# A depthwise convolution shared out anew among TensorE, VectorE, ScalarE and GpSimd

## What is computed

```python
def conformer_conv(h, w_pw1, b_pw1, w_dw, b_dw, ln_g, ln_b, w_pw2, b_pw2):
    u = h @ w_pw1 + b_pw1
    a, gate = jnp.split(u, 2, axis=-1)
    u = a * jax.nn.sigmoid(gate)
    u = lax.conv_general_dilated(          # depthwise, causal, width 31
        u, w_dw[:, None, :], window_strides=(1,), padding=[(CONV_WIDTH - 1, 0)], ...) + b_dw
    u = jax.nn.silu(layernorm(u, ln_g, ln_b))
    return u @ w_pw2 + b_pw2
```

## Time and profile before

| | us |
|---|---|
| median of 3 runs | 1820.41 (1819.27 to 1821.78) |
| span of the profiled execution | 1817.7 |
| TensorE busy in the span | 1765.9 (97%) |
| VectorE busy | 1029.6 (57%) |
| ScalarE busy | 707.8 (39%) |
| GpSimd busy | 172.1 (9%) |

### The profile page before, as it was taken

One profiled execution on the slowest core, in us unless ns is written; L12 is line 12 of the kernel. 1 busy time (PEld: TensorE's weight loads), 2 busy tenths in 40 slices (PEclk: granted clock), 3 DMA queues, 4 the chain that ended last, 5 costly groups with the idle time before them and its releaser, 6 DMA issues.

```text
span 1817.7 us, 21121 instructions
## 1 busy us (share of the span) xinstructions
PE 1765.9 (97%) x8106; PEld 1404.2 (77%) x8106; DVE 1029.6 (57%) x1287; ACT 707.8 (39%) x1095; POOL 172.1 (9%) x128
## 2 busy tenths in 40 slices
PE   7999799999999999999999999989999899999997
PEld 6887588888888878778888888756557778888886
DVE  6998664433444555654424444559856677537753
ACT  5655532212233344332212323465564444324431
POOL 0010010000000100110000004471200200000001
PEclk9999999999999999999999999999999999999998
DMA  5210322322232311132312231523112122322221
GB/s 181 70 47 28 99 94 101 115 95 83 102 118 78 124 70 53 65 105 103 127 70 93 92 127 70 153 73 116 50 62 70 70 93 101 119 70 92 101 96 47
DMA packets 28052, 164.63 MB, mean 91 GB/s; under 512 B 4511, under 2 KB 5675, under 8 KB 11596
## 3 DMA queue, kind: packets, MB, share of 16 engines
q1 hardware_dynamic: 25088, 158.11, 24.7%
q10 hardware_dynamic: 2892, 5.55, 1.0%
HBM read 156.28 MB, written 4.47 MB: 88 GB/s over the span
## 4 chain that ended last, share of the span: by engine, by line
PE 88%; DVE 8%; ACT 2%; issue 1%; POOL 1%; DMA 0%; DVEq 0%; SPq 0%; ACTq 0%; POOLq 0%
PE PS L620 26%; PE PS L622 26%; PE PS L621 26%; PE PS L726 1%; PE PS L727 1%; PE PS L725 1%; DVE W_lo L1821 1%; DVE WK L2266 1%; DVE SSUM L2307 1%; DVE TOP L2264 1%; PE PS L1045 1%; ACT W_hi L1154 1%; POOL ISC L1765 1%; PE PS L1056 1%; DVE PS L2443 0%
## 5 line engine op out<-in xcount | busy, mean ns | idle before, releaser
L620 PE MATMUL PS<-H_hi,W_hi 128*128 128x512 f32 x1600 | 641.6, 401 | 18.3 <-DVE H_lo L1801 14.0
L622 PE MATMUL PS<-H_hi,W_lo 128*128 128x512 f32 x1600 | 626.1, 391 | 0.0
L621 PE MATMUL PS<-H_lo,W_hi 128*128 128x512 f32 x1600 | 625.6, 391 | 0.0
L1154 ACT ACTIVATE W_hi<-W_raw 128x2048 fp32r<-128x2048 f32 (+2 forms) x130 | 262.6, 2020 | 674.2 <-PE PS L622 674.2
L620 PEld LDWEIGHTS PS<-H_hi,W_hi 128*128 128x128 f32 x1600 | 301.9, 189 | 105.1 <-issue 41.2
L1821 DVE TENSOR_TENSOR W_lo<-W_raw,W_hi 128x2048 fp32r<-128x2048 f32 (+2 forms) x130 | 331.2, 2548 | 59.5 <-ACT W_hi L1154 59.1
L622 PEld LDWEIGHTS PS<-H_hi,W_lo 128*128 128x128 f32 x1600 | 301.5, 188 | 64.6
L621 PEld LDWEIGHTS PS<-H_lo,W_hi 128*128 128x128 f32 x1600 | 302.2, 189 | 59.5 <-issue 1.2
L620 PE MATMUL PS<-HID_hi,W_hi 128*128 128x512 f32 x640 | 250.3, 391 | 7.5 <-DVE HID_lo L1962 7.4
L622 PE MATMUL PS<-HID_hi,W_lo 128*128 128x512 f32 x640 | 249.7, 390 | 0.0
L621 PE MATMUL PS<-HID_lo,W_hi 128*128 128x512 f32 x640 | 249.7, 390 | 0.0
(11 more groups left out here) (289 smaller groups left out, 1522.0 us busy)
## 6 DMA issues: line engine op xcount, KB each, us to landing
W_raw<-in_inp SPq DMA_DIRECT2D x13, 1024.0 KB, 4.8
W_raw<-in_pw SPq DMA_DIRECT2D x11, 1024.0 KB, 4.8
W_raw<-in_gu0a SPq DMA_DIRECT2D x11, 1024.0 KB, 4.8
W_raw<-in_gu0b SPq DMA_DIRECT2D x11, 1024.0 KB, 4.8
W_raw<-in_gu1a SPq DMA_DIRECT2D x11, 1024.0 KB, 4.8
W_raw<-in_gu1b SPq DMA_DIRECT2D x11, 1024.0 KB, 4.8
W_raw<-in_gu2a SPq DMA_DIRECT2D x11, 1024.0 KB, 4.8
W_raw<-in_gu2b SPq DMA_DIRECT2D x11, 1024.0 KB, 4.8
```

The lines of the kernel that those rows point to most:

```text
L620: nc.tensor.matmul(dst[:], wh, x_hi[:, k, :], start=(k == first), stop=False)
L621: nc.tensor.matmul(dst[:], wh, x_lo[:, k, :], start=False, stop=False)
L622: return nc.tensor.matmul(dst[:], wl, x_hi[:, k, :], start=False, stop=(k == last))
L1154: nc.scalar.activation(W_hi[b][:, 0:n], W_raw[b][:, 0:n], ACT.Copy).then_inc(w_hi, 1)
```

## The change

The taps are shared by three engines. `PE_TILES` gives TensorE 66 taps: tile 1 whole, the last 9 of tile 5, the last 26 of tile 7. VectorE has 124: tiles 0, 3, 4 and 6 whole. GpSimd has 58 (`POOL_TAPS`): tile 2 whole, 22 of tile 5, 5 of tile 7.

- VectorE's two sums lie in PSUM, in AUX[2] and AUX[3]; only the last tap of a tile writes CV. TensorE's tiles take turns in AUX[0] and AUX[1], and the third waits until the first is copied out.
- For 55 of GpSimd's 58 taps ScalarE makes the product (`scaled_tap`, into one of four buffers TAP in SBUF) and GpSimd adds it to CV. For a tile's tap 0 GpSimd multiplies and adds the bias itself. ScalarE waits for `pool_tap`, the tap four back, before it overwrites a buffer.
- The scaled taps have places in ScalarE's queue by slot (`SCALED_AT`): ten of them between two sigmoids, from slot 50 on; the last four stand ahead of diagonal chunk 9.
- TensorE takes its first tap at slot 64 and one behind every second slot: 32 taps inside the units, 34 behind them, with `bias_products` behind tap 55. The sums of tiles 5, 6 and 7 for the mean are separate matmuls.
- GpSimd's queue: taps of tile 2, mean sums of tiles 0, 2, 3 (it waits for tile 3 of VectorE), taps of tile 5, mean sums of tiles 1 and 4, taps of tile 7.
- `DVE_TAPS` is [5, 8, 9, 16, 16, 16, 16]; behind the last U come 1 tap, `conv_lo`, 20 taps, the join of tile 5, 17 taps, the join of tile 7. `conv_lo` of tile 5 comes in unit 5, that of tile 7 behind the last U.

```diff
-PE_TILES = [(1, 0), (3, 0), (5, 6), (7, 10)]
+PE_TILES = [(1, 0), (5, 22), (7, 5)]
-DVE_TILES = [(0, 31), (2, 31), (4, 31), (5, 6), (6, 31), (7, 10)]
-DVE_TAPS = [5, 8, 21, 24, 24, 24, 24]
+DVE_TILES = [0, 3, 4, 6]
+DVE_TAPS = [5, 8, 9, 16, 16, 16, 16]
+POOL_TILES = [(2, CONV_WIDTH), (5, 22), (7, 5)]
+SCALED = [n for n, (m, t) in enumerate(POOL_TAPS) if t]
-FIRST_TAP = 48
+FIRST_TAP, TAPS_INSIDE = 64, 32
+CHUNK_AT = {g: c for c, g in enumerate([40, 46, 52] + [FIRST_TAP + 2 * CHUNK * (c - 2) for c in range(3, 8)])}
+TAKE_AT = FIRST_TAP + 2 * PE_ENDS[0] + 1
+SCALED_AT = [50 + 3 * k // 2 for k in range(30)] + [101 + 3 * k // 2 for k in range(18)]
-        CVacc = T_hid
+        TAP = [SQ[:, 0, :], SQ[:, 1, :], STD[:], T_hid[:]]
...
+            def scaled_tap(k):
+                n = SCALED[k]
+                m, t = POOL_TAPS[n]
+                if t == 1:
+                    act.wait_ge(glu_made, m + 1)
+                if k >= len(TAP):
+                    act.wait_ge(pool_tap, SCALED[k - len(TAP)] + 1)
+                nc.scalar.activation(TAP[k % len(TAP)], U[:, m, t:t + SEQ], ACT.Copy,
+                                     scale=vec("w_dw", t * DT + m)).then_inc(act_scaled, 1)
...
+            def taps(x):
+                m, end = POOL_TILES[x]
+                for n in range(POOL_ENDS[x] - end, POOL_ENDS[x]):
+                    t = POOL_TAPS[n][1]
+                    if t == 0:
...
+                        nc.gpsimd.tensor_scalar(CV[:, m, :], U[:, m, 0:SEQ], vec("w_dw", m), vec("b_dw", m),
+                                                ALU.mult, ALU.add).then_inc(pool_tap, 1)
+                        continue
+                    k = SCALED.index(n)
+                    pool.wait_ge(act_scaled, k + 1)
+                    pool.wait_ge(pool_tap, n)
+                    nc.gpsimd.tensor_tensor(CV[:, m, :], CV[:, m, :], TAP[k % len(TAP)], ALU.add).then_inc(pool_tap, 1)
...
             def conv(count, upto):
...
-                    dst = (CV[:, m, :], CVacc[:])[t % 2]
+                    acc = AUX[2 + t % 2][:]
...
-                        i = nc.vector.scalar_tensor_tensor(out=dst, in0=src, scalar=w, in1=dst, op0=ALU.mult, op1=ALU.add)
+                        dst = CV[:, m, :] if t == CONV_WIDTH - 1 else acc
+                        i = nc.vector.scalar_tensor_tensor(out=dst, in0=src, scalar=w, in1=acc, op0=ALU.mult, op1=ALU.add)
...
             conv(1, DT)
-            conv_lo(3)
-            conv(9, DT)
-            conv_joined(2)
+            conv_lo(2)
+            conv(20, DT)
+            conv_join(1)
             conv(len(todo), DT)
-            conv_joined(3)
+            conv_join(2)
```

More of the change, by code:

```diff
@@ L378, in build @@
         r_copied = sem("r_copied")
-        y_scaled = sem("y_scaled")
-        t_pool = sem("t_pool")
+        act_scaled = sem("act_scaled")
+        pool_tap = sem("pool_tap")
         x_pool = sem("x_pool")
@@ L720, in conv_tap @@
                     pe.wait_ge(r_copied, COPIED_NORMS.index(MIX0) + 1)
+                    if p == 2:
+                        pe.wait_ge(conv_pe_taken, 1)
                 if x == 0:
@@ L754, in _ @@
                             token_spread(AUX[1], r_ps)
-                        if g >= FIRST_TAP:
-                            conv_tap(g - FIRST_TAP)
-            for n in range(SLOTS * L.n - FIRST_TAP, len(PE_TAPS)):
+                        if g >= FIRST_TAP and g % 2 == 0:
+                            conv_tap((g - FIRST_TAP) // 2)
+            for n in range(TAPS_INSIDE, len(PE_TAPS)):
                 conv_tap(n)
-            bias_products()
-            pe.wait_ge(ln_sum, 7)
+                if n == 55:
+                    bias_products()
+            pe.wait_ge(acc_free, L.n)
+            pe.wait_ge(ln_sum, len(MEAN_POOL) - 1)
             nc.tensor.matmul(PS[0][:], ones, SSUM[:], start=True, stop=False)
-            pe.wait_ge(conv_made, 6)
+            pe.wait_ge(conv_made, MADE.index(5) + 1)
+            nc.tensor.matmul(PS[0][:], ones, CV[:, 5, :], start=False, stop=False)
+            pe.wait_ge(conv_made, MADE.index(6) + 1)
+            nc.tensor.matmul(PS[0][:], ones, CV[:, 6, :], start=False, stop=False)
+            pe.wait_ge(conv_made, MADE.index(7) + 1)
             nc.tensor.matmul(PS[0][:], ones, CV[:, 7, :], start=False, stop=True).then_inc(ln_sum_ready, 1)
@@ L1287, in beside_pw1 @@
                         split_hi(act, L, At(j - 1))
-                    if j - 1 in (1, 3, 5):
-                        conv_hi((j - 2) // 2)
+                    if j - 1 in (1, 5):
+                        conv_hi((j - 1) // 4)
                 if g in CHUNK_AT:
                     diagonals(CHUNK_AT[g])
-                if g in TAKE_AT:
-                    take_conv(TAKE_AT[g])
+                if g == TAKE_AT:
+                    take_conv()
+                if g in SCALED_AT:
+                    scaled_tap(SCALED_AT.index(g))
             def take_bias(g):
@@ L1302, in _ @@
             glu_gate(L.n - 1)
-            conv_hi(3)
+            conv_hi(2)
             act.dma_start(onehot[:], a["onehot"]).then_inc(tab_in, 16)
             act.dma_start(table[0:BUCKETS, :], a["rel_bias"]).then_inc(tab_in, 16)
-            for g, c in CHUNK_AT.items():
-                if g >= SLOTS * L.n:
-                    diagonals(c)
+            for k in range(len(SCALED_AT), len(SCALED) - 4):
+                scaled_tap(k)
+            diagonals(8)
+            for k in range(len(SCALED) - 4, len(SCALED)):
+                scaled_tap(k)
+            diagonals(9)
+            diagonals(10)
             split_hi(act, L, At(L.n - 1))
@@ new lines, in mean_add @@
+            def mean_add(i):
+                m = MEAN_POOL[i]
+                if m == 1:
+                    pool.wait_ge(conv_pe_taken, 1)
+                else:
+                    pool.wait_ge(conv_made, MADE.index(m) + 1)
+                pool.wait_ge(ln_sum, i - 1)
+                nc.gpsimd.tensor_tensor(SSUM[:], SSUM[:], CV[:, m, :], ALU.add).then_inc(ln_sum, 1)
+            taps(0)
+            pool.wait_ge(conv_made, 1)
+            pool.wait_ge(pool_tap, POOL_ENDS[0])
+            nc.gpsimd.tensor_tensor(SSUM[:], CV[:, 0, :], CV[:, 2, :], ALU.add).then_inc(ln_sum, 1)
@@ L1719, in add_squares @@
+            mean_add(2)
+            taps(1)
+            mean_add(3)
+            mean_add(4)
+            pool.wait_ge(ln_sum, len(MEAN_POOL) - 1)
+            pool.wait_ge(acc_ready, 2 * (L.base + L.n))
+            nc.gpsimd.memset(table[BUCKETS:BUCKETS + 1, :], NEG).then_inc(pads_set, 1)
+            pool.wait_ge(pads_set, 2)
+            taps(2)
             def add_squares(norm):
@@ L1851, in _ @@
             HALO = CONV_WIDTH - 1
-            todo = [(m, t) for m, end in DVE_TILES for t in range(end)]
+            todo = [(m, t) for m in DVE_TILES for t in range(CONV_WIDTH)]
             taken_steps = [0]
@@ L1928, in _ @@
                     split_lo(L, At(j))
-                    if j in (1, 3, 5):
-                        conv_lo(j // 2)
+                    if j in (1, 5):
+                        conv_lo(j // 4)
                     if j == 0:
```

64 lines of the change are left out of this document (25 added, 39 removed).

## The result

The changed kernel takes 1810.58 us (median of 4 runs, 1810.43 to 1810.79) against 1820.42 (median of 4 runs, 1819.27 to 1821.78): ratio 0.9949, 95% interval 0.9937 to 0.9961. The forecast was 1808.7 in a range of 1802 to 1816.

A forecast was written before the change was run, and what follows sets the result against it. TensorE and VectorE were taken as full, TensorE setting the end, VectorE close behind. Subtracting the mean at 170.0 instead of 181.7 gains 11.7: 1817.7 - 11.7 = 1806.0, plus 2.7 median offset, 1808.7 us; range 1802 to 1816.

The forecast's parts named there:

- Price of a tap in PSUM: VectorE's taps with sums in PSUM cost the same as in SBUF: 0.665 us start to start, bounds 0.60 and 0.77.
- Rivals D and E: D: PSUM taps 0.77 apart, 1822 us, chance 0.08. E: taps meet GpSimd's sums at the port, 1861, chance 0.05.
- Ports of VectorE: U, W_lo and conv_lo wait for GpSimd at the shared SBUF port, 0.65 us each, 7.5 us in all.
- Each of them will meet a sum under way: Each U, W_lo and conv_lo finds GpSimd adding; VectorE waits 0 to 1.3 us, taken as 0.65.
- Late sigmoids: VectorE waits for sigmoids behind products in ScalarE's queue: 3.7, 0, 0.6, 3.0, 1.2 us in units 3 to 7, 8.5 in all.
- The walk: Unit-by-unit timing of the convolution stage from unit 2 to 7, T_g of unit 7 at 135.1 us.
- TensorE's end: TensorE stands 11 us before tile 7's taps, loses 2.1 to half clock, ends at 163.4, 165.2 with two channel sums.
- The last join: VectorE is late last, by 3 us: last join done at 168.7, mean subtracted from 170.0 instead of 181.7.
- Rival C: TensorE's clock falls in its last wait of 2.9 us, slowing channel sums and squares: +5 us, 1814, chance 0.12.
- Behind it nothing is changed: After the mean's subtraction nothing changes, so the stage's gain of 11.7 us comes off the span whole.
- A, B and C: A: as forecast, 1808.7 us, chance 0.58. B: kinder balance, 1803, 0.17. C: clock falls in last wait, 1814, 0.12.

The follow-up runs named there:

- sigmoid_early: Changed kernel with only ScalarE's queue reordered: 7 products ahead of unit 3's sigmoid, then 9 instead of 10 between two sigmoids; 1801.48 us.
- chunks_behind: Changed kernel with diagonal chunks 3, 4 and 6 right behind a sigmoid and its W_hi, 5 mid-unit, 7 behind the last sigmoid; 1805.67 us.
- short_sums: Changed kernel with 496 of the 512 columns of each of GpSimd's 55 sums left out, all instructions and waits kept; 1795.46 us.
- tuned: reordered with bias_products behind TensorE's last tap, 8 products instead of 9 and chunk 7 ahead of the last sigmoid, one more VectorE tap in unit 6; 1799.02 us.
- reordered: Changed kernel with the queue orders of sigmoid_early and chunks_behind, and chunks 8, 9, 10 between products, three by three; 1805.09 us.
- filled_wait: tuned with three useless matmuls behind the sum of tile 5, in TensorE's wait ahead of the sum of tile 6; 1798.65 us.

## Why the prediction was right, point by point

- **Price of a tap in PSUM** (0.665, bounds 0.60 and 0.77): right. The 112 taps take 752 ns and stand 0.66 apart (four of them 2.73). Rivals D and E fell. The estimate from the Trainium skill, VectorE: DVE Perf Modes, section on the TRN2 errata, 8 us more, is not borne out.
- **Ports of VectorE** (7.5 us): too large. U lost 0.86 + 0.27 + 0.13, conv_lo 1.11 + 0.27, W_lo nothing: 2.6. The step that failed is "Each of them will meet a sum under way". U releases GpSimd, and from there both count: four taps are 2.63 us, so W_lo starts at 88.15, just behind a sum that ends at 88.07 (86.78 + 1.29), and the next sum waits instead. All four W_lo start 0.1 us behind the end of a sum. That this is the reason for the pattern is argued from the rows, no run set it apart; in `sigmoid_early` one of the four was held (2.73).
- **Late sigmoids** (3.7, 0, 0.6, 3.0, 1.2 = 8.5 us): too small, 13.2. Units 3, 5 and 6 were right within 0.6; units 4 and 7 were missed. The walk let the sigmoid wait for GpSimd's sum alone and priced the chunk of diagonals only in ScalarE's total. A chunk stands behind the last product that waits, so its 3.5 us come on top. This is the step of the walk that failed. `chunks_behind` confirms it for unit 4. `short_sums` leaves 2.0 of the 13.2 us and `sigmoid_early` 3.2, so GpSimd's pace and the order of the queue together made nearly all of it.
- That these two errors cancel (15.8 measured, 16.0 forecast) is luck: one cause was charged three times too high, the other a third too low. Because of it T_g of unit 7 comes at 133.63 (135.1 forecast) and its conv_lo ends at 141.9 (141.2).
- **TensorE's end** (163.4, and 165.2 with two sums): 165.0 and 166.7. It stood 12.1 (11) and lost 2.7 us to half clock (2.1): 16 taps at full clock would end at 141.99 + 11.1 = 153.1, and bias_products starts at 155.85.
- **The last join** (done at 168.7, mean from 170.0): 169.2 and 170.6. VectorE last, as said; a little of GpSimd was better than said (opening multiply 0.77, not 1.1), and chunk 9 came in time.
- **Rival C** (half clock in the last wait): not here, where the wait was 1.69 us and not 2.9. With waits of 2.98 and 3.14 us `short_sums` and `tuned` have it, so with the 2.9 us of the walk the clock would probably have halved here too (no run of this kernel shows it), and the walk gave no reason for it to stay full.
- **The remaining 1.9 us.** "Behind it nothing is changed" holds for the work, not for its time: the rest is 2.1 us longer. Comparing the starts of the same W_lo in both kernels, 0.7 are lost at pw2, whose clock rises 5.6 us after TensorE resumes and 4.1 in the kernel before, 0.2 more by 1417, 0.9 between 1417 and 1444, where both kernels have a half-clock stretch of different length, and 0.3 behind that. Against that, the median lies 1.9 above the span instead of 2.7. The sum: 1806.0 + 0.6 + 2.1 = 1808.7 is the span.
- **Slips in the working.** T_g of unit 7 adds up to 116 + 15.1 + 1.3 + 3.0 = 135.4, not 135.1; and A, B and C alone make 0.87, so no part of D is in it. Neither moves the forecast by more than 0.3 us.

## What to carry to other kernels

When one in-order engine feeds both a slow consumer and the critical path, list, for each instruction that the critical path waits for, what stands ahead of it in the queue: each entry that waits for the slow consumer, and all work behind the last such entry. Move what you can behind the critical instruction. Here moving products in one list shortened the stage by 7.7 us (9.1 in the median) with no work taken away. VectorE's sums in PSUM cost nothing per tap (the first instruction of a tile took 0.81 instead of 0.55 us) and took VectorE out of GpSimd's way; without them the same split is 43 us slower. Judge a change by the stage that it touches, since a few us come and go elsewhere with TensorE's clock.

## What the runs showed of the hardware

- The clock in TensorE's last wait: waits of 0.59, 1.69 and 2.38 us left it full, waits of 2.98 and 3.14 us found it halved. Ahead of tile 7's taps and among them, `sigmoid_early` has waits of 2.79 and 2.53 us behind which the clock fell 0.4 and 0.7 us after TensorE had resumed. In `tuned` it fell at about 157.5, 2.9 us after the engine had stopped at 154.6; in the kernel after it fell at 133.9, 4.0 us after the end of the last tap at 129.9; in `short_sums` 2.3 us after the stop, in `reordered` 5.2 us after it. Time of standing alone does not say when it falls.
- Behind the same wait of 7.39 us ahead of pw2 the clock came back 2.9 us after TensorE had resumed in `reordered`, 4.1 in the kernel before, 4.3 in `tuned`, 5.6 in the kernel after and 5.9 in `filled_wait` (worked out from the granted clock of the slice in which it rose, 0.63, 0.75, 0.81, 0.53 and 0.74). Half of the difference is lost or won.
- Unchanged work took from 1633.6 to 1639.6 us in the eleven kernels. Where the difference was followed, it lay in stretches at half clock that one kernel had and the other had not.
- VectorE and GpSimd, both with two SBUF inputs, alternate at 1.70 us a pair, more than either takes alone (0.66 and 1.43) and less than both together.
